# Two-layer encoder trunk on one core: the third weight sum of each Strassen block made by an adding DMA from GpSimd, one product moved, the engines' lists ordered anew

## The chip, the cores and the metric

The kernel runs on one core of a Trainium2 chip. The metric is the device time of one execution in microseconds. Engines: PE (TensorE), DVE (VectorE), ACT (ScalarE), POOL (GpSimd), and SP (SyncE), which issues nearly all DMAs. All weights are read from HBM in float32.

## The reference, cut to what matters

```python
def _swiglu(h, w_gate, w_up, w_down):
    return (jax.nn.silu(h @ w_gate) * (h @ w_up)) @ w_down

for l in range(DEPTH):                       # DEPTH = 2
    x = x + 0.5 * _swiglu(_rms_norm(x, ffn1_norm[l]), ffn1_w_gate[l], ffn1_w_up[l], ffn1_w_down[l])
    h = _rms_norm(x, mix_norm[l])
    ...                                      # convolution branch and attention branch, gated sum, w_out
    x = x + 0.5 * _swiglu(_rms_norm(x, ffn2_norm[l]), ffn2_w_gate[l], ffn2_w_up[l], ffn2_w_down[l])
return x
```

x is 256 x 1024; w_gate and w_up are 1024 x 2816, w_down is 2816 x 1024. There are four such feed-forward nets (FFNs), two in each layer, with the mixer between the two of a layer. The change touches the FFNs alone. The mixer matters here for one thing: attention needs the sine and cosine of positions times frequencies (the rotary key), and its RMS norm needs a root.

## The kernel before, in words

**Precision.** A product of float32 matrices is made of three passes on PE (`products`): the high part of the left with the high part of the right, high with low, low with high. So each weight unit (128 partitions x 2048 floats, 1 MB) is first split: ACT writes its rounded copy `whi` (`rounded`, line 1344), then DVE writes the remainder `wlo` = raw - `whi` (`remainder`, line 1854). A unit on PE is 24 matmuls of 512 columns for each 128 rows of x with gate/up weights, 12 + 12 with a down unit, 12 for a block product.

**Units and rings.** The units of a layer have one fixed order (`FFN_UNITS`, from `PRODUCTS`); `whi_ready`, `wlo_ready` and `unit_free` count them in this order. `whi` and `wlo` are rings of 6 units, `raw`, into which SP loads, is a ring of 3 (`place` waits until the unit three loads earlier is split, and `summed` for sums that still read it).

**An FFN** runs over 11 chunks of 256 hidden columns. A plain chunk c is `gate_up(c, 0)`, `gate_up(c, 1)` (two row tiles), and the down products of chunk c - 2. Chunks 4, 5 and chunks 7, 8 are done as one *block* each, in Strassen's way, with seven half-size products instead of eight: `strassen(4)` and `strassen(7)`. Its weights are quarters of w_gate and w_up: B11 (upper half of w_gate), an upper quarter of w_up, B22 (lower half of w_up), B21 (lower half of w_gate). DVE makes the sums T1 = B11 + upper w_up, T2 = T1 + B22, T3 = upper w_up + B22, T4 = T2 + B21 in place in two buffers, `chain[0]` (T1, T2, T4; it shares memory with `htok`) and `chain[1]` (T3; with `heads`), by `add` at line 2002. A sum is then split like any unit (`sum_of` on ACT, `of_chain` on DVE). The order of products on PE was B11, down of chunk c - 2, T1, T2, B22, B21, T3, T4, down of chunk c - 1.

**Order.** Each engine runs its list of steps in order; the lists of SP, ACT and DVE are written out by hand in each engine's `ffn` (SP from line 585, ACT from 1543, DVE from 2090), and every step waits on semaphores. `silu`, `mul`, `split_planes`, the transposing DMA `turn`, `join`, `round_joined` and `rest_joined` bring a chunk's hidden values from gate/up to the operand of its down product; `keep`, `up_first`, `gate_first` and their like gather a block's products.

**POOL** has in the FFNs only the roots of the norms (`root`, line 697, in `norm(l, n)`) and, in the first FFN of each layer, the range reduction for sine and cosine: 16 products (line 722) and 34 further steps, each followed by a small product (line 715) behind a wait. After these comes `norm(l, 1)`, the two roots of the mixer's norm. On DVE `norm_apply(l, 1, 0)` (line 1902) waits for the first of them, and behind it in DVE's list stands `mul(10, 1)` (line 1963), for which the last chunk's transposes on PE (`turn`, line 1028) wait.

Of the kernel before, what the change touches and what calls it, by code (L numbers as in the profile page):

```python
# [17 lines left out]
ALU = mybir.AluOpType  # L18
# [8 lines left out]
P = 128  # L27
# [6 lines left out]
FC = 256  # L34
# [25 lines left out]
PRODUCTS = ("B11", "D0", "T1", "T2", "B22", "B21", "T3", "T4", "D1")  # L60
# [32 lines left out]
SUM = {"T1": 1, "T2": 1, "T3": 1, "T4": 1}  # L93
# [77 lines left out]
def trunk(nc, a):  # L171
    with ExitStack() as ctx:
# [286 lines left out]

        block = ctx.enter_context(nc.Block())  # L460

        @block.sync
        def _(sp):
            def summed(l, u):
# [29 lines left out]

            def quarter_of(w, l, c, h):

                return w[l, 4 * h * P:4 * (h + 1) * P, c * FC:c * FC + CW].rearrange("(k p) n -> p k n", p=P)
# [68 lines left out]
            def ffn(l, f):  # L566
# [43 lines left out]
                lower_load(l, f, 4, "B22")  # L610
                turn(2)
                lower_load(l, f, 4, "B21")
# [11 lines left out]
                turn(5)  # L624
                turn(6)
                down(l, f, 6)
# [6 lines left out]
                down(l, f, 8)  # L633
                turn(8)
                down(l, f, 9)
                turn(9)
                down(l, f, 10)
# [50 lines left out]
        def _(pool):  # L688
# [14 lines left out]

            for l in range(DEPTH):
                norm(l, 0)

# [114 lines left out]
                norm(l, 2)  # L821


        @block.tensor
        def _(pe):
# [45 lines left out]
            def ffn(l, f):  # L871
# [45 lines left out]
                def strassen(c):  # L917
# [422 lines left out]
        def _(act):  # L1340
# [92 lines left out]
            def ffn(l, f):  # L1433
# [103 lines left out]
                silu(1, 0)  # L1537
                down_split(0)
                silu(1, 1)
# [6 lines left out]
                gate_split(3, 1)  # L1546
                down_split(1)
                round_joined(1)
                split_planes(2, 0)
                first_of(4, "B11")  # L1550
                silu(2, 1)
                split_planes(2, 1)
                down_split(2)
                sum_of(4, "T1")
                silu(3, 0)
                round_joined(2)
                silu(3, 1)
# [3 lines left out]
                split_planes(3, 0)  # L1561
                split_planes(3, 1)
                lower(4, "B21")
                sum_of(4, "T3")
                keep(4, 1, "T1")
                sum_of(4, "T4")
                keep(4, 2, "T2")
                down_split(3)
                gate_split(6, 0)
                round_joined(3)  # L1570
                keep(4, 3, "T3")
                block_silu(4, 0)
                gate_split(6, 1)
                split_planes(4, 0)
                block_silu(4, 1)
# [13 lines left out]
                sum_of(7, "T2")  # L1589
                keep(7, 0, "B11")  # L1590
                lower(7, "B22")
# [926 lines left out]
```

## Time and profile before

| | |
|---|---|
| median of 3 runs | 1025.89 us (1024.97, 1025.89, 1027.45) |
| profiled execution | 1025.66 us, span 1023.9 us |
| PE busy | 1018.2 us (99%), 4905 matmuls |
| DVE busy | 846.4 us (83%) |
| ACT busy | 660.8 us (65%) |
| POOL busy | 330.8 us (32%) |
| granted PE clock | 1.00 in every slice |
| HBM read | 192.9 MB, 189 GB/s over the span |

The profiled execution takes 1.8 us beside its span, and lies 0.2 us under the median. A matmul's start is recorded, its end is modelled, and each starts before the one ahead of it has ended; the distance between starts is what a matmul costs. "Idle before" is an engine's idle time ahead of a group with the releaser that ended it.

### The profile page before, as it was taken

To read this page: it belongs to the slowest core of one execution; us is meant where nothing else is said; L and a number is where in the kernel's file an instruction comes from. 1 tells how busy PE (TensorE), PEld (TensorE's weight loads), DVE (VectorE), ACT (ScalarE), POOL (GpSimd) and SP (SyncE) were. 2 spreads that over 40 slices of the span, in tenths; PEclk is the share of its full clock that TensorE was granted. 3 is DMA by queue.
4 is the path that set the end of the run, shared out by engine and by line. 5 is a ranking of instruction groups with operands and counts; after the bars stand their busy time and mean duration, and the time that the engine had idled before them with its cause. 6 is when DMAs were issued, how large, how long until landed. Compare 5 with 4: busy or idle time off the path is not lost.

```text
span 1023.9 us, 13331 instructions
## 1 busy us (share of the span) xinstructions
PE 1018.2 (99%) x4905; PEld 853.9 (83%) x4905; DVE 846.4 (83%) x1008; ACT 660.8 (65%) x836; POOL 330.8 (32%) x258
## 2 busy tenths in 40 slices
PE   9999999999999999999999999999999999999998
PEld 6888888998888888888888888889988888888887
DVE  6999977698976898888679889866999678988972
ACT  6767665576874575766557666647778556666761
POOL 2999400138850100000049990001589300000000
PEclk9999999999999999999999999999999999999999
DMA  8968578555544596748749574975366365947491
GB/s 278 309 191 277 162 209 274 160 185 176 207 161 128 182 328 183 244 140 234 228 154 339 166 226 135 274 248 174 127 214 226 123 173 185 331 140 233 158 240 42
DMA packets 175185, 208.99 MB, mean 204 GB/s; under 512 B 64112, under 2 KB 129936, under 8 KB 175120
## 3 DMA queue, kind: packets, MB, share of 16 engines
q1 hardware_dynamic: 173904, 206.03, 64.9%
q10 hardware_dynamic: 1216, 2.11, 0.7%
q8 instruction: 39, 0.64, 0.2%
q14 instruction: 26, 0.21, 0.1%
HBM read 192.90 MB, written 1.05 MB: 189 GB/s over the span
## 4 chain that ended last, share of the span: by engine, by line
PE 98%; ACT 1%; DVE 1%; DMA 0%; issue 0%; POOL 0%; ACTq 0%
PE bank L829 30%; PE bank L831 30%; PE bank L830 30%; PE bank L966 1%; PE bank L1128 1%; PE bank L1137 1%; PE bank L1158 1%; PE bank L868 0%; PE bank L1136 0%; PE bank L1160 0%; PE bank L836 0%; DMA cacc<-in_ffn_norm 0%; DVE htok L1902 0%; DVE x L1950 0%; ACT htok L1357 0%; PE bank L1146 0%
## 5 line engine op out<-in xcount | busy, mean ns | idle before, releaser
L1854 DVE TENSOR_TENSOR wlo<-raw,whi 128x2048 fp32r<-128x2048 f32 (+2 forms) x136 | 308.9, 2283 | 21.0 <-ACT whi L1344 21.0
L1344 ACT ACTIVATE whi<-raw 128x2048 fp32r<-128x2048 f32 (+2 forms) x160 | 302.9, 1910 | 25.3 <-DMA raw<-in_ffn_w_down 16.5
L829 PE MATMUL bank<-whi,hThi 128*128 128x512 f32 (+1 forms) x816 | 316.1, 387 | 0.0
L831 PE MATMUL bank<-whi,hTlo 128*128 128x512 f32 (+1 forms) x816 | 311.4, 382 | 0.0
L830 PE MATMUL bank<-wlo,hThi 128*128 128x512 f32 (+1 forms) x816 | 311.3, 381 | 0.0
L697 POOL TENSOR_TENSOR small<-small,expo 128x1 f32<-128x1 f32 (+3 forms) x20 | 30.0, 1505 | 470.5 <-DVE small L1895 432.9
L831 PEld LDWEIGHTS bank<-whi,hTlo 128*128 128x128 f32 x816 | 153.2, 188 | 29.6
L829 PEld LDWEIGHTS bank<-whi,hThi 128*128 128x128 f32 x816 | 153.3, 188 | 28.8
L830 PEld LDWEIGHTS bank<-wlo,hThi 128*128 128x128 f32 x816 | 153.4, 188 | 28.4
L829 PE MATMUL bank<-whi,gThi 128*128 128x512 f32 (+1 forms) x416 | 162.3, 390 | 0.0
L831 PE MATMUL bank<-whi,gTlo 128*128 128x512 f32 (+1 forms) x416 | 161.2, 388 | 0.0
L830 PE MATMUL bank<-wlo,gThi 128*128 128x512 f32 (+1 forms) x416 | 161.1, 387 | 0.0
L811 POOL TENSOR_TENSOR wlo<-raw,whi 128x2048 fp32r<-128x2048 f32 x24 | 110.1, 4608 | 21.1 <-ACT whi L1344 21.0
L2233 DVE SCALAR_TENSOR_TENSOR bank<-shared,vec,bank 128x256 f32<-128x256 f32 x240 | 98.1, 478 | 0.2
L831 PEld LDWEIGHTS bank<-whi,gTlo 128*128 128x128 f32 x416 | 78.1, 188 | 16.1
L829 PEld LDWEIGHTS bank<-whi,gThi 128*128 128x128 f32 x416 | 78.1, 188 | 15.8 <-issue 0.3
L830 PEld LDWEIGHTS bank<-wlo,gThi 128*128 128x128 f32 x416 | 78.2, 188 | 15.5
L1854 DVE TENSOR_TENSOR wlo<-htok,whi 128x2048 fp32r<-128x2048 f32 x32 | 73.2, 2287 | 10.7 <-ACT whi L1344 10.7
L715 POOL TENSOR_TENSOR small<-expo 128x1 f32<-128x1 f32 x72 | 75.0, 1041 | 5.9
L1344 ACT ACTIVATE whi<-htok 128x2048 fp32r<-128x2048 f32 x32 | 61.2, 1911 | 22.1 <-DVE htok L2002 17.4
L1497 ACT ACTIVATE qkT<-gates 128x512 uint16<-128x512 uint16 x80 | 48.5, 623 | 29.9 <-DVE gates L1963 14.8
L1458 ACT ACTIVATE gates<-bank 128x512 f32<-128x512 f32 x32 | 19.1, 596 | 61.6 <-PE bank L831 61.6
(201 smaller groups left out, 1359.0 us busy)
## 6 DMA issues: line engine op xcount, KB each, us to landing
raw<-in_ffn_w_down SPq DMA_DIRECT2D x88, 512.0 KB, 4.7
raw<-in_ffn_w_gate SPq DMA_DIRECT2D x68, 512.0 KB, 4.2
raw<-in_ffn_w_up SPq DMA_DIRECT2D x68, 512.0 KB, 5.2
raw<-in_w_in SPq DMA_DIRECT2D x48, 512.0 KB, 4.9
htok<-in_ffn_w_gate SPq DMA_DIRECT2D x16, 512.0 KB, 6.1
heads<-in_ffn_w_up SPq DMA_DIRECT2D x16, 512.0 KB, 6.8
raw<-in_w_out SPq DMA_DIRECT2D x16, 512.0 KB, 4.6
raw<-in_w_in SPq DMA_DIRECT2D x8, 544.0 KB, 5.2
```

The source lines that it names most:

```text
L697: return nc.gpsimd.tensor_tensor(out, in_, expo[:, :].to_broadcast([P, out.shape[-1]]), ALU.pow)
L715: nc.gpsimd.tensor_tensor(small[:, 95:96], expo[:, :], expo[:, :], ALU.mult)
L811: nc.gpsimd.tensor_tensor(wlo[:, slot(u, RING), 0:n], raw[:, raw_slot(l, u), 0:n], whi[:, slot(u, RING), 0:n].bitcast(F32), ALU.subtract). ...
L829: nc.tensor.matmul(out, lh, rh, start=start, stop=False, skip_group_check=skip)
L830: nc.tensor.matmul(out, lh, rl, start=False, stop=False, skip_group_check=skip)
L831: return nc.tensor.matmul(out, ll, rh, start=False, stop=stop, skip_group_check=skip)
L966: ins = nc.tensor.matmul(bank[:, 4 + t, :], left[:, 4 * h + k, t * P:(t + 1) * P], view(right, h, 2048, 4)[:, k, :], start=first and (h, k ...
L1344: nc.scalar.activation(whi[:, slot(u, RING), 0:USED[u]], src, ACT.Copy).then_inc(whi_ready, 1)
L1458: nc.scalar.activation(kept[(0, 2, 1, 3)[i]], bank[:, 5 if i == 1 else 4, :], ACT.Copy).then_inc(kept_ready, 1)
L1497: nc.scalar.activation(planes[:, :, :, t, :], words, ACT.Copy).then_inc(planes_ready, 1)
L1854: nc.vector.tensor_tensor(wlo[:, slot(u, RING), 0:n], src, whi[:, slot(u, RING), 0:n].bitcast(F32), ALU.subtract).then_inc(wlo_ready, 1)
L2233: ins = nc.vector.scalar_tensor_tensor(out=o, in0=i, scalar=w, in1=o, op0=ALU.mult, op1=ALU.add)
```

## The change

The sum T3 moves from DVE to a DMA that adds to its destination. POOL, once the upper quarter of w_up has landed in `chain[1]` and T1 (which reads it) is made, issues two DMAs of 512 KB, which read the lower half of w_up from HBM a second time and add it to `chain[1]`. `sum_ready["T3"]` then counts 32 for each block, and SP no longer waits for T3 before it reuses the place of B22. In POOL's list the waits and issues of both blocks stand directly behind the roots of the FFN's norm, and so ahead of the range reduction. On PE the T1 product goes ahead of the down product of chunk c - 2, and the two change places in the order of units. The lists of SP, ACT and DVE are in a new order. The diff, cut:

```diff
-PRODUCTS = ("B11", "D0", "T1", "T2", "B22", "B21", "T3", "T4", "D1")
+PRODUCTS = ("B11", "T1", "D0", "T2", "B22", "B21", "T3", "T4", "D1")
...
-SUM = {"T1": 1, "T2": 1, "T3": 1, "T4": 1}
+SUM = {"T1": 1, "T2": 1, "T3": 32, "T4": 1}
...
@@ SP, summed @@
                 if name == "B22":
                     sp.wait_ge(sum_ready["T2"], per_block(l, f, c))
-                    sp.wait_ge(sum_ready["T3"], per_block(l, f, c))
@@ SP, list of the FFN (chunks 2 to 4; the rest is reordered alike) @@
                 down(l, f, 0)
+                gate_up(l, f, 3, 0)
+                chain_load(l, f, 4, 0)
                 turn(0)
-                gate_up(l, f, 3, 0)
                 gate_up(l, f, 3, 1)
+                turn(1)
                 down(l, f, 1)
-                turn(1)
-                chain_load(l, f, 4, 0)
                 chain_load(l, f, 4, 1)
...
                 gate_up(l, f, 6, 1)
+                chain_load(l, f, 7, 0)
+                down(l, f, 4)
+                turn(4)
                 chain_load(l, f, 7, 1)
-                down(l, f, 4)
-                chain_load(l, f, 7, 0)
-                turn(4)
                 down(l, f, 5)
@@ POOL @@
+            def add_rows(l, f, c, name):
+
+                done = per_block(l, f, c)
+                if name == "T3":
+                    pool.wait_ge(chain_landed[1], done * 32)
+                    pool.wait_ge(sum_ready["T1"], done)
+                    dst, src = chain[1], quarter_of(wu[f], l, c, 1)
+                dst = dst.rearrange("p (k n) -> p k n", k=4)
+                for k in (0, 2):
+                    nc.gpsimd.dma_start(dst[:, k:k + 2, :], src[:, k:k + 2, :],
+                                        accum_op=ALU.add).then_inc(sum_ready[name], 16)
+
+            def sums(l, f):
+
+                add_rows(l, f, 4, "T3")
+                add_rows(l, f, 7, "T3")
+
             for l in range(DEPTH):
                 norm(l, 0)
+                sums(l, 0)
...
                 norm(l, 2)
+                sums(l, 1)
@@ PE, strassen @@
-                    down(c - 2, 0)
-                    down(c - 2, 1)
                     if c == BLK[0]:
                         pe.wait_ge(mixed_ready, l * 2 + f + 1)
                     block_product(c, "T1", 5, mixed_T(1, 1))
+                    down(c - 2, 0)
+                    down(c - 2, 1)
@@ ACT, list of the FFN @@
                 if (l, f) != (0, 0):
                     gate_split(1, 0)
+                    silu(0, 0)
                     gate_split(1, 1)
                     norm_squares(l, 2 * f, 1)
+                    silu(0, 1)
                     gate_split(2, 0)
-                    silu(0, 0)
-                    silu(0, 1)
                 split_planes(0, 0)
                 split_planes(0, 1)
                 gate_split(2, 1)
                 silu(1, 0)
+                silu(1, 1)
                 down_split(0)
-                silu(1, 1)
...
                 silu(6, 0)
-                down_split(5)
                 sum_of(7, "T1")
                 silu(6, 1)
+                round_joined(5)
+                down_split(5)
+                sum_of(7, "T2")
+                lower(7, "B22")
+                keep(7, 0, "B11")
                 split_planes(6, 0)
-                round_joined(5)
+                keep(7, 1, "T1")
+                lower(7, "B21")
                 split_planes(6, 1)
...
@@ DVE @@
-                def add_T3(c):
-                    dve.wait_ge(sum_ready["T1"], per_block(l, f, c) * SUM["T1"])
-                    add(c, "T3", lower_raw(c, "B22"))
...
                 mixed_rows()
+                mul(1, 0)
                 gate_split(2, 1)
                 join(0)
+                rest_joined(0)
+                mul(1, 1)
                 down_split(0)
-                mul(1, 0)
-                mul(1, 1)
-                rest_joined(0)
...
                 of_chain(7, "B11")
+                mul(6, 0)
                 add_T1(7)
                 rest_joined(4)
-                down_split(5)
-                mul(6, 0)
-                mul(6, 1)
                 join(5)
                 of_chain(7, "T1")
+                add_T2(7)
                 rest_joined(5)
-                add_T2(7)
-                add_T3(7)
+                mul(6, 1)
+                down_split(5)
                 of_chain(7, "T2")
                 lower(7, "B22")
+                lower(7, "B21")
                 add_T4(7)
-                lower(7, "B21")
                 of_chain(7, "T3")
```

## Rows read from the trace of the kernel before

**Rows 1.** page, parts 1 and 2: busy time and clock of the span

```profile
PE 1018.2 (99%) x4905; PEld 853.9 (83%) x4905; DVE 846.4 (83%) x1008; ACT 660.8 (65%) x836; POOL 330.8 (32%) x258
...
PEclk9999999999999999999999999999999999999999
```

**Rows 2.** who PE waited for: us in total, times, longest

```profile
PE bank L836 <- DVE zero L2432: 1.2, 1, 1.2
```

**Rows 3.** timeline of PE in block 7, first FFN: start us, us, line, operation

```profile
105.87 0.39 PE L829 MATMUL bank<-whi,gThi 128*128 128x512 f32 x1
...
114.03 0.39 PE L829 MATMUL bank<-whi,gThi 128*128 128x512 f32 x1
...
130.35 0.39 PE L829 MATMUL bank<-whi,sThi 128*128 128x512 f32 x1
```

**Rows 4.** groups of DVE by form: busy us, mean ns, idle before

```profile
L2002 DVE TENSOR_TENSOR heads<-heads,raw 128x2048 f32<-128x2048 f32 x8 | 18.3, 2281 | 0.0
```

**Rows 5.** timeline of DVE in the first FFN, around block 7

```profile
99.83 2.29 DVE L2002 TENSOR_TENSOR htok<-htok,heads 128x2048 f32<-128x2048 f32 x1
102.03 0.69 DVE L1861 TENSOR_TENSOR gTlo<-gates,gThi 128x512 fp32r<-128x512 f32 x1
```

**Rows 6.** timeline of ACT in the same stretch

```profile
100.63 0.47 ACT L1443 ACTIVATE gates<-bank,small 128x256 f32<-128x256 f32 x1 [1.83 <-PE bank L831]
101.00 1.91 ACT L1344 ACTIVATE whi<-raw 128x2048 fp32r<-128x2048 f32 x1
```

**Rows 7.** DMA issues: KB each, median us to landing

```profile
heads<-in_ffn_w_up SPq DMA_DIRECT2D x16, 512.0 KB, 6.8
```

**Rows 8.** timeline of POOL: the range reductions, and the roots behind them

```profile
22.25 0.19 POOL L720 CAST small<-posi 128x2 f32<-128x2 int32 x1
...
89.15 0.25 POOL L735 TENSOR_TENSOR ang<-ang 128x32 f32<-128x32 f32 x1
...
91.46 0.75 POOL L735 TENSOR_TENSOR ang<-ang 128x32 f32<-128x32 f32 x1
...
112.95 2.10 POOL L715 TENSOR_TENSOR small<-expo 128x1 f32<-128x1 f32 x1
174.28 0.57 POOL L697 TENSOR_TENSOR small<-small,expo 128x1 f32<-128x1 f32 x1 [59.23 <-DVE small L1895]
...
679.54 0.57 POOL L697 TENSOR_TENSOR small<-small,expo 128x1 f32<-128x1 f32 x1 [63.72 <-DVE small L1895]
```

**Rows 9.** windows: PE, PEld, DVE, ACT, POOL busy us (instructions), clock, DMA share, GB/s

```profile
22.00:44.00 22.00, 22.00 (x99) 18.21 (x98) 21.26 (x19) 17.43 (x19) 20.98 (x20) 1.00 0.96 280
44.00:115.00 71.00, 71.00 (x315) 58.80 (x314) 66.04 (x46) 45.14 (x44) 66.99 (x68) 1.00 0.74 239
106.00:140.00 34.00, 34.00 (x152) 28.15 (x151) 31.71 (x23) 21.82 (x21) 8.58 (x10) 1.00 0.47 146
140.00:174.30 34.30, 34.30 (x154) 28.37 (x153) 24.64 (x20) 19.93 (x21) 0.02 (x1) 1.00 0.97 289
...
611.00:646.00 35.00, 35.00 (x156) 29.00 (x155) 32.35 (x23) 22.56 (x22) 4.43 (x9) 1.00 0.49 151
646.00:679.50 33.50, 33.50 (x150) 27.69 (x150) 23.91 (x20) 19.19 (x20) 0.00 (x0) 1.00 0.93 289
```

**Rows 10.** timelines of DVE and PE at the end of the first FFN

```profile
177.75 0.48 DVE L1963 SCALAR_TENSOR_TENSOR gates<-bank,small,gates 128x256 f32<-128x256 f32 x1 [1.58 <-ACT gates L1443]
...
179.57 0.38 PE L1028 MATMUL bank<-ident,gates 128*128 128x128 f32 x2
```

**Rows 11.** timelines of ACT, DVE and PE, start of the second FFN

```profile
354.14 0.47 ACT L1443 ACTIVATE gates<-bank,small 128x256 f32<-128x256 f32 x1 [2.31 <-POOL small L697]
...
356.53 2.61 DVE L2034 TENSOR_TENSOR gates<-gates 128x512 f32<-128x512 f32 x4
359.12 2.29 DVE L1854 TENSOR_TENSOR wlo<-raw,whi 128x2048 fp32r<-128x2048 f32 x1
...
364.87 0.39 PE L829 MATMUL bank<-whi,hThi 128*128 128x512 f32 x1
```

More of the change, by code:

```diff
@@ L610, in ffn @@
                 lower_load(l, f, 4, "B22")
+                lower_load(l, f, 4, "B21")
                 turn(2)
-                lower_load(l, f, 4, "B21")
                 down(l, f, 3)
@@ L624, in ffn @@
                 turn(5)
+                down(l, f, 6)
                 turn(6)
-                down(l, f, 6)
                 gate_up(l, f, 9, 0)
@@ L633, in ffn @@
                 down(l, f, 8)
+                down(l, f, 9)
                 turn(8)
-                down(l, f, 9)
+                down(l, f, 10)
                 turn(9)
-                down(l, f, 10)
             def block_of(l, u, w, r0, k, c0, n):
@@ L1546, in ffn @@
                 gate_split(3, 1)
+                round_joined(1)
                 down_split(1)
-                round_joined(1)
+                silu(2, 1)
                 split_planes(2, 0)
                 first_of(4, "B11")
-                silu(2, 1)
                 split_planes(2, 1)
+                silu(3, 0)
+                sum_of(4, "T1")
+                split_planes(3, 0)
+                silu(3, 1)
+                round_joined(2)
                 down_split(2)
[L1554 to L1557, printed above, removed]
                 sum_of(4, "T2")
@@ L1582, in ffn @@
                 silu(6, 0)
[L1583 removed]
                 sum_of(7, "T1")
                 silu(6, 1)
+                round_joined(5)
[3 more added lines that the diff above has]
+                keep(7, 0, "B11")
                 split_planes(6, 0)
[L1587 removed]
+                keep(7, 1, "T1")
+                lower(7, "B21")
                 split_planes(6, 1)
[L1589 to L1592 removed]
                 sum_of(7, "T3")
[L1594 removed]
+                sum_of(7, "T4")
                 keep(7, 2, "T2")
[L1596 removed]
                 down_split(6)
+                round_joined(6)
                 gate_split(9, 0)
[L1599 removed]
+                gate_split(9, 1)
                 keep(7, 3, "T3")
                 block_silu(7, 0)
[L1602 removed]
                 block_silu(7, 1)
@@ L1606, in ffn @@
                 down_split(7)
+                gate_split(10, 0)
                 split_planes(8, 0)
+                silu(9, 0)
                 split_planes(8, 1)
                 round_joined(7)
-                gate_split(10, 0)
-                silu(9, 0)
                 gate_split(10, 1)
                 silu(9, 1)
+                down_split(8)
                 split_planes(9, 0)
                 split_planes(9, 1)
-                down_split(8)
+                down_split(9)
                 round_joined(8)
-                down_split(9)
                 c = NCH - 1
@@ L2135, in ffn @@
                 of_chain(4, "T3")
+                of_chain(4, "T4")
                 join(3)
-                of_chain(4, "T4")
-                up_first(4)
                 down_split(3)
                 rest_joined(3)
+                gate_split(6, 0)
+                up_first(4)
                 gate_first(4)
-                gate_split(6, 0)
+                block_mul(4, 0)
                 up_second(4)
-                block_mul(4, 0)
                 gate_second(4)
@@ L2167, in ffn @@
                 of_chain(7, "T4")
-                gate_first(7)
                 down_split(6)
                 rest_joined(6)
+                up_first(7)
+                gate_split(9, 0)
                 up_second(7)
-                gate_split(9, 0)
+                gate_first(7)
                 gate_second(7)
-                up_first(7)
                 block_mul(7, 0)
@@ L2178, in ffn @@
                 down_split(7)
+                gate_split(10, 0)
                 join(7)
+                mul(9, 0)
                 rest_joined(7)
-                gate_split(10, 0)
-                mul(9, 0)
+                gate_split(10, 1)
                 mul(9, 1)
                 join(8)
-                gate_split(10, 1)
-                rest_joined(8)
                 down_split(8)
                 down_split(9)
+                rest_joined(8)
                 c = NCH - 1
```

43 lines of the change are left out of this document (18 added, 25 removed).

## Prediction, made before the changed kernel was run

> **What bounds the kernel now.** I read the busy times first, then who PE waited for, then the distances between PE's starts, then the slack of each thing that PE consumes in the stretch that is changed.
>
> PE is busy 1018.2 of 1023.9 us at the full clock [rows 1]. PE's own list of waits has three entries, each a single wait in the first 15 us of the kernel; the longest is 1.2 us [rows 2]. So the question in each FFN is whether its matmuls start at their own pace or are stretched. In block 7 of the first FFN, PE starts the down products of chunk 4 at 105.87, the next product but one at 114.03, T3 at 130.35 [rows 3]. Between the first and the last lie 24 (down 4) + 12 (B11) + 24 (down 5) + 12 (T1) + 12 (T2) + 12 (B22) + 12 (B21) = 108 matmuls of 512 columns: (130.35 - 105.87) / 108 = 0.2267 us each. From 105.87 to 114.03 it is 8.16 / 36 = 0.2267 us: the same pace to the last digit. PE has no gap there, whatever DVE, ACT and the DMAs do. The windows of the first and third FFN say the same: 315 matmuls in 71.00 us, 152 in 34.00, 156 in 35.00 [rows 9] are 0.224 to 0.225 us each (one that crosses an edge counts in full); a stretch with a stall of 1 us would hold 4 fewer. The change takes no matmul away and adds none. What it can give back from the FFNs is nothing; all that it can do is to make something late that now is in time. That decides the sign, and the rest of this text asks for lateness.
>
> **The change part by part.**
>
> *Eight sums leave DVE.* They are 8 instructions of 2.281 us, 18.3 us in all [rows 4]. PE waited for none of them, so they are worth 0. They come back as time in which DVE waits for PE.
>
> *T3 by DMA, and when it has to be there.* Take block 7, the tighter one. DVE adds T1 from 99.83 on [rows 5], right behind the remainder of B11. In the new list `mul(6, 0)` stands ahead of it, and needs the `silu` that ACT makes at 100.63 for 0.47 us [rows 6], because PE has only then finished the products. So: silu done 101.1, mul (0.48, [rows 10]) 101.6, T1 (2.29) 103.9. `rest_joined(4)` behind it takes 0.69 [rows 5], to 104.6; PE wants it at 105.87 [rows 3]: 1.2 us to spare, no stall. The T3 product stays at 130.35, because T1 and the down product ahead of it only change places. Before it lie the remainder on DVE (2.28) and the rounding on ACT (1.91, [rows 6]): T3 must have landed by 130.35 - 2.28 - 1.91 - 0.1 = 126.1. Nothing at all moves if it has landed when ACT gets there; working ACT's and DVE's new lists forward with these durations gives 120. From T1 at 103.9 that is 16 us free of any effect and 22 us until PE waits. In block 4 the same working gives T1 at 54.5 and windows of 18 and 25 us.
>
> How long do the two adding DMAs take? No row shows one, nor any DMA from POOL. The nearest is the plain load of the same 512 KB into the same buffer: 6.8 us from issue to landing [rows 7], median of 16. Lower end: both overlap as the plain ones do, 7 to 8 us. Upper end: the destination is read as well as written, and the two run one after the other at double the time: 4 x 6.8 = 27 us, 5 us more than PE's limit in block 7 and 2 more in block 4. I take 8 to 14, nearer the plain load, since the 16 DMA engines are less than half busy there (share 0.47 from 106 to 140 us, [rows 9]). Cost 0; at the upper end 4 x (5 + 2) = 28 us.
>
> The Trainium skill ("DMA: Bandwidth & Descriptors", section "Anatomy of one DMA — SWDGE (gpsimd) path") gives 2.0 us + bytes / 436e3 for one DMA from GpSimd, an estimate of 3.2 us for 512 KB; it says nothing of an adding one. By it T3 would be in time as well.
>
> *POOL's list: what the new waits hold up.* This is the part with a price. The issues stand ahead of the range reduction, and the second pair waits for T1 of block 7. So in layer 1 the reduction no longer starts at 22.25 but at about 103.9 + 2 issues. A DMA issue on POOL is in no row: at least about 0, like POOL's short operations, at most the 6.8 us of a whole load [rows 7], if POOL were held until the data have landed. I take 1 us, nearer the short end, because an issue only describes the transfer. Start 106. The reduction took from 22.25 to 115.05, 92.8 us [rows 8]. Moved by its whole length it would end at 199, 25 us after the root that now starts at 174.28 [rows 8]. That would stall DVE at `norm_apply`, then `mul(10, 1)`, then PE.
>
> But its length isn't fixed. Its operations take 2.1 us beside a long DVE operation (112.95, as long as the 2.28 us that DVE holds) and 0.29 us when DVE is idle or reads PSUM: eight starts from 89.15 to 91.46 [rows 8]. Count by windows [rows 9]: from 22 to 115 POOL did 20 + 68 = 88 operations while DVE did 19 + 46 = 65 and was idle 0.74 + 4.96 = 5.70 us. 5.70 / 0.29 = 20 operations in idle time, the other 68 are 1.05 for each DVE operation. Now the new place, 106 to 174.3: DVE does 23 + 20 = 43 operations and is idle 2.29 + 9.66 = 11.95 us, giving 45 + 41 = 86 operations. T3's add, now gone from there, gives 2.28 / 0.29 - 1.05 = 7 more: 93, where 88 are needed. The reduction ends some 3 us before its root is due. In layer 2 everything comes 505.3 us later (root at 679.54 for 174.28, [rows 8]): start 611, DVE 43 operations and 2.65 + 9.59 = 12.24 us idle to 679.5 [rows 9], 45 + 42 + 7 = 94 for 89. So the cover holds, but it is thin: 5 operations. Behind it come 1.34 us of slack: `mul(10, 1)` ends at 178.23, PE wants it at 179.57 [rows 10]. Later than that each operation still missing costs 0.29 us, since DVE then stands still and no longer holds POOL up.
>
> The Trainium skill ("SBUF — State Buffer", section "Who interferes with whom") has the rule behind these rows: DVE and GpSimd share one port pair, held for a whole instruction, a DVE operation with two SBUF inputs shutting out a GpSimd operation that reads SBUF; the 2.1 us beside 0.29 us agree. The same page speaks against the change: GpSimd writes the descriptors of its DMAs itself, and is locked out while DVE runs in a two-port mode. If that held for each long operation, an issue would wait one of them out.
>
> *The orders.* T1 before down 5: T1 is wanted at 114.03 [rows 3]; forward from 103.9, ACT rounds it to 105.9 and DVE has the remainder at 108.1, 5.9 us early. The down product goes back by 2.72 us, so its unit and operand have more time. The tightest place that I find is the second half of chunk 2's weights in FFNs 2 to 4. Now: mixed rows to 359.1, remainder from 359.12 to 361.41, wanted by PE at 364.87 [rows 11]. New: silu to 354.61 (bound by POOL's root, [rows 11]), then `gate_split(2, 0)` on ACT to 356.5 and on DVE to 358.8, mul 359.2, mixed rows (2.61) 361.8, mul(1, 0) 362.5, remainder 364.8. It is ready 0.1 us before PE wants it. I charge 0.1 us for each of four FFNs, 0.4 in all; 0 to 2 is possible. SP's list: it loses one wait and no load of it moves by more than a few us; the last down unit is now asked for ahead of a transpose, which helps slightly and off the path.
>
> Sum: 0 (sums) + 0 (DMA) + 0 (POOL) + 0.4 (order) on the profiled 1025.66 us gives 1026.1; on the median, 0.2 us higher, 1026.3. I say 1026.2.
>
> **The rivals.**
>
> *POOL is late (slower).* The point from which it decides: 5 operations of surplus and 1.34 / 0.29 = 4.6 of slack, at 0.94 operations per us in the stretch from 106 to 140 (32 in 34 us), is 10 us. If the two issues of block 7 hold POOL for more than about 12 us, near the upper end of 2 x 6.8, PE stalls at the end of the first FFN of each layer. For 20 us: (18 x 0.94 - 9.6) x 0.29 = 2.1 us a layer, 4 in all: 1030. If each issue had to wait out one long DVE operation (2.28 us), the pair would take 6.6 us and stay under the point. Chance 0.09.
>
> *T3 lands late (slower).* From 22 us after T1 on. At the upper end, +28 us: 1054; a few us beyond the limit in block 7 alone, +4 to +12: 1034. Against it: a share of the DMA engines of 0.47. Chance 0.07.
>
> *The new lists starve PE somewhere (slower).* 0.1 us of spare at chunk 2, 1.2 us at `rest_joined(4)`. Half a microsecond short in each FFN at two places gives 4 us: 1030. Chance 0.07.
>
> *DVE was the bound after all (faster).* Then 18 us come back: 1008. Against it speaks the even 0.2267 us. Chance 0.02; another 0.01 for less than that.
>
> **How the numbers follow.** A measurement of this kernel can tell about 0.2% (2 us) from no change. Forecast case 0.74, 1025 to 1028, which is within 0.2% of 1025.89. The three slower rivals have 0.23. Faster by over 0.2%: 0.03; within: 0.74; slower: 0.23. The range reaches from 1024.8 (the lowest run of before less a little) up to 1030.5, which takes in the late POOL and short stalls and leaves out the late T3.
>
> **What would show each step.** The remaining DVE additions are 24 instead of 32, and DVE's busy time falls by 18 us with the end unmoved. PE's starts stay at 0.2267 us through both blocks. ACT's wait for T3 is short or absent; the POOL operations run from about 106 to about 172 us, more of them at 0.2 to 0.3 us, and the root behind them starts at 174.3. If instead `norm_apply` (line 1902) waits longer for POOL in the list of waits than now, POOL is late; if line 1344 waits for a DMA ahead of T3, the sum is late; if PE shows waits for `wlo` at chunk 2, it is the lists. A PE pace other than 0.2267 us in the FFNs would overturn the whole argument.

## The result, and the profile after

The changed kernel takes 1052.37 us (median of 4 runs, 1049.15 to 1055.2) beside 1025.43 us for the kernel before on the same chip: a ratio of 1.0259, 95% interval 1.0241 to 1.0276. It is 26.9 us slower, where 1026.2 and no change that can be measured was forecast, and it lies far outside the range. Its profiled run took 1051.78 us, of which the span is 1050.0, 26.1 us more than before; this span is taken apart below. In the comparisons that follow, one execution of e4 (2082 us) and one of the kernel before (1128 us) fell in a slow state, and the ratios are made without them. The page of the profiled run, to be held against [rows 1]:

```profile
span 1050.0 us, 13343 instructions
PE 1028.5 (98%) x4905; PEld 856.9 (82%) x4905; DVE 829.6 (79%) x1000; ACT 660.5 (63%) x836; POOL 300.7 (29%) x274
PEclk9999999999999999989999999999999999999999
PE 50%; POOL 13%; DVE 13%; DMA 10%; issue 7%; ACT 5%; SPq 2%; ACTq 0%; DVEq 0%; POOLq 0%
```

DVE lost 17 us of work, as the change meant, and the end came 26 us later. The chain of work that ended last (the last line) is only half PE now, with DMA, DVE and POOL in it. PE is still "98% busy", since its idle time rose only from 5.7 to 21.5 us; its busy time rose too, by 10.3 us, of which half is a slower pace (below). The list of waits says more. For PE, where [rows 2] had nothing beyond the start:

```profile
PE bank L847 <- DVE gTlo L1879: 8.7, 4, 2.5
PE bank L847 <- DVE wlo L1872: 5.2, 4, 3.1
PE bank L886 <- DVE htok L1920: 1.9, 2, 1.2
```

And for those PE waits for (us in total, times, longest):

```profile
DVE gates L1996 <- DMA qkT<-qkT: 52.8, 16, 9.8
ACT gThi L1523 <- DVE gates L1996: 51.6, 18, 8.6
POOL heads L712 <- issue: 49.4, 8, 10.5
```

The first of these stood at 3.6 us in 4 times, 1.3 at the longest, in the kernel before (its line was 1978 there). `join` (line 1996) waits for the transposing DMA `turn`, then ACT waits for `join`, then PE for DVE's remainder.

**Where the 26.1 us of span lie.** I summed what PE's starts lie further apart than 0.2267 us, over all matmuls of 512 columns. Eleven starts (one is that of a transpose on PE between two of them) came over 0.3 us late, 16.4 us together (none before). Behind the first 8 us, 46 starts stand 0.35 to 0.5 us apart, where the kernel before has 16: 5.9 us more. The two waits at the mixer's norm are 1.9 us. That makes 24.2 of 26.1 us; the rest is spread thin. The loss comes FFN by FFN: 6.7, 8.3, 6.6 and 4.6 us.

The first chunk shows how it starts. SP's list in the first FFN, the kernel before and then the changed one:

```profile
26.63 1.34 SPq L537 DMA_TRANSPOSE qkT<-qkT  x1
29.99 0.39 SPq L484 DMA_DIRECT2D raw<-in_ffn_w_gate  x1
```

```profile
30.29 0.38 SPq L487 DMA_DIRECT2D raw<-in_ffn_w_gate  x1
30.71 0.51 SPq L487 DMA_DIRECT2D raw<-in_ffn_w_up  x1
31.27 1.02 SPq L512 DMA_DIRECT2D htok<-in_ffn_w_gate  x2
32.40 1.67 SPq L536 DMA_TRANSPOSE qkT<-qkT  x1
```

The load `gate_up(3, 0)` can't go before 30 us in either kernel, because its place of `raw` isn't free. The transpose now stands behind it, and goes at 32.40 rather than 26.63. It also lands behind 2 MB of loads just issued: 7.3 us after its issue rather than 4.9. In the kernel before it landed at 31.54 and `join(0)` was made at 34.62, without a wait. DVE, in order:

```profile
39.72 0.76 DVE L1996 COPY gates<-qkT 128x1024 uint16<-128x1024 uint16 x1 [4.33 <-DMA qkT<-qkT]
...
63.76 0.76 DVE L1996 COPY gates<-qkT 128x1024 uint16<-128x1024 uint16 x1 [2.72 <-DMA qkT<-qkT]
...
73.60 0.68 DVE L1879 TENSOR_TENSOR gTlo<-gates,gThi 128x512 fp32r<-128x512 f32 x1
```

Chunks 0 and 2 are joined late. From 63.76 on DVE works without a gap, and the remainder of chunk 2 (`rest_joined`, 73.60), with five steps of its list between it and the join, comes when PE has run dry:

```profile
71.80 0.39 PE L849 MATMUL bank<-whi,sTlo 128*128 128x512 f32 x1
74.34 0.50 PE L847 MATMUL bank<-whi,gThi 128*128 128x512 f32 x1 [2.15 <-DVE gTlo L1879]
...
75.85 0.63 PE L847 MATMUL bank<-whi,gThi 128*128 128x512 f32 x1
76.27 0.63 PE L848 MATMUL bank<-wlo,gThi 128*128 128x512 f32 x1
```

After the stall the starts go on at about 0.23 us apart for 1.5 us, and then stand 0.427 us apart for eight matmuls. From 75.8 to 80 us the granted clock was 0.59; the eight are at the lower of PE's two clock levels, 1.2 GHz. The worst place is block 7 of the second FFN, where `join(5)` waits longest and PE then runs at half clock (windows: PE busy and count, clock, DMA share, GB/s):

```profile
452.72 0.74 DVE L1996 COPY gates<-qkT 128x1024 uint16<-128x1024 uint16 x1 [9.80 <-DMA qkT<-qkT]
```

```profile
456.00:462.00 6.00, 5.94 (x15) 0.54 0.54 87
462.00:480.00 18.00, 18.00 (x81) 1.00 0.71 217
```

The clock costs 26 such matmuls x 0.2 = 5.2 us of the 26.1; they are most of the 5.9 us above.

**POOL.** Its two pairs of adding DMAs in the first FFN, the start of the reduction, and the root behind it:

```profile
60.70 1.35 POOL L712 DMA_DIRECT2D heads<-in_ffn_w_up  x1 [38.13 <-DVE htok L2020]
67.01 1.23 POOL L712 DMA_DIRECT2D heads<-in_ffn_w_up  x1 [4.96 <-issue]
110.04 1.22 POOL L712 DMA_DIRECT2D heads<-in_ffn_w_up  x1 [41.80 <-DVE htok L2020]
117.72 1.23 POOL L712 DMA_DIRECT2D heads<-in_ffn_w_up  x1 [6.46 <-issue]
118.47 0.82 POOL L737 CAST small<-posi 128x2 f32<-128x2 int32 x1
...
181.62 0.57 POOL L696 TENSOR_TENSOR small<-small,expo 128x1 f32<-128x1 f32 x1
```

An issue costs 1.2 us, but the second stands still until the first has landed (110.04 + 7.3 = 117.3, then 117.72; at 443.00 in the second FFN the first took 11.4 us, and the second went at 454.72). The reduction took 63 us from 118.5 to 181.6, in place of the 92.8 us of [rows 8].

### The profile page after: what moved, and what is told of

Read it like the earlier page. It is cut to its first block, busy times and chain, and to the rows that moved or that the text cites. A ratio compares the mean times of both kernels' runs of the same rounds, so it can differ in the third digit from the quotient of the medians.

```text
span 1050.0 us, 13343 instructions
## 1 busy us (share of the span) xinstructions
PE 1028.5 (98%) x4905; PEld 856.9 (82%) x4905; DVE 829.6 (79%) x1000; ACT 660.5 (63%) x836; POOL 300.7 (29%) x274
## 4 chain that ended last, share of the span: by engine, by line
PE 50%; POOL 13%; DVE 13%; DMA 10%; issue 7%; ACT 5%; SPq 2%; ACTq 0%; DVEq 0%; POOLq 0%
PE bank L847 15%; PE bank L848 15%; PE bank L849 15%; DMA qkT<-qkT 8%; DVE wlo L1872 7%; POOL ang L739 4%; POOL small L732 4%; ACT whi L1362 2%; DMA raw<-in_ffn_w_down 2%; DVE htok L2020 2%; POOL ang L751 2%; POOL small L696 1%; SPq L487 1%; POOL ang L752 1%; ACT qkT L1515 1%
## 5 line engine op out<-in xcount | busy, mean ns | idle before, releaser
L847 PE MATMUL bank<-whi,gThi 128*128 128x512 f32 (+1 forms) x416 | 165.0, 397 | 10.9 <-DVE gTlo L1879 8.7
L712 POOL DMA_DIRECT2D heads<-in_ffn_w_up x16 | 19.8, 1239 | 356.7 <-DVE htok L2020 307.3
L849 PEld LDWEIGHTS bank<-whi,gTlo 128*128 128x128 f32 x416 | 79.0, 190 | 16.8
L1996 DVE COPY gates<-qkT 128x1024 uint16<-128x1024 uint16 x40 | 30.2, 754 | 53.2 <-DMA qkT<-qkT 52.8
L1461 ACT ACTIVATE gates<-bank,small 128x256 f32<-128x256 f32 x56 | 26.3, 470 | 58.5 <-PE bank L849 45.5
```

Of the source, the lines that this page charges most:

```text
L847: nc.tensor.matmul(out, lh, rh, start=start, stop=False, skip_group_check=skip)
L849: return nc.tensor.matmul(out, ll, rh, start=False, stop=stop, skip_group_check=skip)
L1461: nc.scalar.activation(sgate[:, t, :], gu_bank(c, t)[:, 0:FC], ACT.Silu, scale=rs[:, t:t + 1]).then_inc(silu_ready, 1)
L1996: nc.vector.tensor_copy(g_turned.bitcast(U16).rearrange("p (n b) -> p b n", b=2), turned.rearrange("p (b j) r -> p b (j r)", b=2)).then_in ...
```

## The experiments

All times are medians. The kernel before measured 1025.3 to 1025.9 us in these comparisons.

**Which part costs.** Theory S: transposes behind loads in SP's list. Theory D: the adding DMA. Theory P: the new place of T1 with the new lists of ACT and DVE. Four kernels, the first being the changed kernel with SP's old list:

```diff
 # SP's list, after -> e1 (all its lines as before), for instance
-                gate_up(l, f, 3, 0)
-                chain_load(l, f, 4, 0)
                 turn(0)
+                gate_up(l, f, 3, 0)
```

> The changed kernel with SP's list of the kernel before: each transposing DMA is issued again ahead of the loads that the change put in front of it; all else as changed. Theory S (the transposes land late because SP issues them behind 1 to 3 MB of loads, DVE's join waits for them, and its lists pass the lateness on to PE): DVE's wait for the transposes falls from 52.8 us to under 15, PE's waits from about 16 us to under 4, time 1026 to 1032 us. Theory D (the adding DMA takes the DMA engines from the transposes): still 1045 to 1055. Theory P (T1 ahead of the down product, or the new lists of ACT and DVE, are too tight by themselves): 1040 or more.

Measured: 1028.19 us, ratio 1.0020 (1.0010 to 1.0029). DVE's wait for the transposes fell from 52.8 to 19.3 us (under 15 was expected), and PE waits only in the start. The execution whose trace is kept took 1026.30 us, the shortest of ten, so it doesn't show where the 2.5 us of the median lie.

The second is the reverse, the kernel before with the changed list of SP and nothing else:

> The kernel before with nothing changed but SP's list, taken from the changed kernel. Theory S: join waits for the transposes as in the changed kernel (tens of us in sum), PE starves in block 4 and 7, time 1038 to 1055 us. Theories D and P: no adding DMA and no moved product here, so 1025 to 1028.

Measured: 1048.52 us, 1.0217 (1.0193 to 1.0241). So the list alone, without an adding DMA and with every product in its old place, costs 22.9 us. But these are not the changed kernel's stalls. Added over the four FFNs, PE's starts fall behind those of the kernel before by 2.9 us up to the end of block 7 (24.0 in the changed kernel) and by 16.9 us from there to the FFN's end (2.4 in the changed kernel). What PE waits for most is `mul(10, 1)`, ahead of the last chunk's transposes on PE:

```profile
PE bank L1028 <- DVE gates L1963: 9.2, 4, 2.5
```

Ahead of it DVE stood 4.6 us in the first FFN for the transposing DMA of chunk 8, which the new list also puts behind a load. So e2 shows that SP's list alone makes transposes late and costs time; that it costs nearly the same time is luck. The third is the DMA alone:

```diff
 # before -> e3: add_rows and sums on POOL as in the change, and on DVE
-                add_T3(4)
-                add_T3(7)
```

> The kernel before with T3 made by POOL's two adding DMAs, the waits and issues ahead of the range reduction as in the change; T3's add is gone from DVE; all lists otherwise and PE's order as before. Theory S: nothing is late, 1025 to 1028 us, the first root of the mixer's norm late by 0 to 3 us at most. Theory D: the transposes are late here too, 1038 to 1052.

Measured: 1025.72 us, 0.9999 (0.9989 to 1.0009). Theory D falls, and 18 us less work on DVE bring nothing, as PE was dense. ACT waited twice for the adding DMA ahead of T3, 0.6 and 0.8 us, without any effect on PE. Its POOL:

```profile
103.02 1.22 POOL L712 DMA_DIRECT2D heads<-in_ffn_w_up  x1 [37.48 <-DVE htok L2020]
110.05 1.23 POOL L712 DMA_DIRECT2D heads<-in_ffn_w_up  x1 [5.82 <-issue]
...
172.69 0.19 POOL L732 TENSOR_TENSOR small<-expo 128x1 f32<-128x1 f32 x1
174.60 0.57 POOL L696 TENSOR_TENSOR small<-small,expo 128x1 f32<-128x1 f32 x1 [1.72 <-DVE small L1913]
```

The reduction ends 1.7 us before its root. The fourth is the changed kernel with T3 back on DVE:

```diff
 # after -> e4
-                sums(l, 0)
-                sums(l, 1)
+                add_T3(4)      # DVE, behind down_split(2), ahead of rest_joined(2)
+                add_T3(7)      # DVE, behind down_split(5)
```

> The changed kernel with T3 added by DVE again (ahead of the remainder of T2), no DMA from POOL; SP's list and all else as changed. Theory S: still 1045 to 1060 us. Theory D: 1026 to 1032.

Measured: 1060.93 us, 1.0333 (1.0316 to 1.0350), 8.6 us above the changed kernel and just above what either theory had. Once the transposes are late, taking the sum off DVE is worth 8.6 us; the same is worth nothing in e3. Most of it can be read at one place: the add of 2.28 us stands here ahead of `rest_joined(2)`, which in the kernel before was ahead of it, and PE's waits for that remainder grow from 8.7 us (2.5 at the longest) to 16.5 (4.3). No run has the add behind it, so what the DMA is worth with the better order stays open.

The other half of theory P, T1 ahead of the down product in the kernel before:

> Edit: the kernel before, with the T1 product ahead of the down product of chunk c - 2 on PE and in the order of units, and only those steps of ACT's and DVE's lists exchanged that this order asks for; SP's list of the FFN as before, T3 on DVE. Theory S (only the transposes' place in SP's list costs): T1 is wanted 24 matmuls (5.4 us) earlier and the spare shrinks from there, PE keeps 0.2267 us: 1025 to 1027. Rival P (T1 is too early for the old list of DVE, where its sum stands behind other steps): a stall of 0.5 to 2 us in each of 8 blocks, 1029 to 1040, seen as a wait of PE for wlo ahead of the product with gThi of mixed rows.

Measured: 1025.48 us, 0.9998 (0.9989 to 1.0007): no cost that can be measured.

**Which transposes.** In the changed list those of chunks 0 and 2 stand behind loads that they were ahead of. That of chunk 5 has the same loads ahead of it as before, but `chain_load(7, 1)` has moved from ahead of `turn(4)` to behind it, so that 4 MB rather than 3 MB are issued between the two transposes. Each was put back alone, then all three:

```diff
 # after -> f1                          # after -> f2
+                turn(0)                -                lower_load(l, f, 4, "B21")
                 gate_up(l, f, 3, 0)                     turn(2)
                 chain_load(l, f, 4, 0) +                lower_load(l, f, 4, "B21")
-                turn(0)
 # after -> f3: chain_load(l, f, 7, 1) to ahead of down(4), chain_load(l, f, 7, 0) to behind it;
 # turn(4) and turn(5) then stand behind the same loads as before
 # f4: f1, f2 and f3 together
```

> Edit: the changed kernel, but in SP's list the transposing DMA of chunk 0 goes ahead of the two loads behind which it now waits. Everything else, the later transposes among it, stays as changed. Theory S (each transpose issued behind loads brings its own lateness): the transpose is issued near 26.6 us again instead of 32.4 and lands in about 5 us, join(0) no longer waits, and the stall of 1.0 us near 43.5 us goes together with its slow matmuls: 3 to 8 us of the 26 come back, 1044 to 1049. Theory L (lateness is inherited: what is late at chunk 0 makes chunks 2 and 5 late): nearly all comes back, 1027 to 1034. Theory O (chunk 0 is harmless, 2 and 5 carry it): 1050 to 1053.

> Edit: the changed kernel, but the transposing DMA of chunk 2 goes ahead of the load of B21 of block 4 again, behind B22's alone. Theory S: its landing falls from 7.6 to about 4.6 us, the stall of 2.3 us near 71.8 us in the first FFN (and the like in the other three) goes or shrinks to below 1 us: 6 to 12 us come back, 1040 to 1046. Theory L: next to nothing comes back, since the lateness starts at chunk 0: 1048 to 1053.

> Edit: the changed kernel, but the two chain loads of block 7 have their old places and order in SP's list (1 ahead of down(4), 0 behind it), so that the transposes of chunks 4 and 5 are not behind the second of them. Theory S: chunk 5's transpose lands in 7 to 9 us rather than 9.5 to 14, and the stall of 3.3 us near 452 us shrinks: 4 to 12 us come back, 1040 to 1048. Theory L: 1048 to 1053. A rival in this place alone: the landing of chunk 5's transpose is set by the two down units and by POOL's adding DMA, not by the chain load; then under 3 us come back.

> Edit: the three edits on SP's list together; all other places of the changed list (turn(1) ahead of down(1), turn(6) behind down(6), turn(8), turn(9), turn(7)) stay as changed. Theory S: these three transposes carry the loss: 1027 to 1032. If it comes out above 1036, other places of SP's list count as well, and which is to be read from the transposes' landings. If the sum of what the three give back one by one is well below what they give together, a stall stays as long as any one of them is late (the lists pass it on); if it is above, they overlap.

Measured: f1 1037.69 (1.0111, 1.0095 to 1.0127), f2 1043.87 (1.0179, 1.0162 to 1.0195), f3 1039.38 (1.0127, 1.0099 to 1.0156), f4 1026.11 (1.0007, 0.9998 to 1.0017). The three carry all of the changed kernel's loss: with them back, and the adding DMA, the early T1, the new lists of ACT and DVE and the rest of SP's new list kept, the time is that of the kernel before. PE's waits in f4 are those of the start, and DVE's for transposes are short:

```profile
PE bank L854 <- DVE zero L2444: 1.2, 1, 1.2
```

```profile
DVE gates L1996 <- DMA qkT<-qkT: 12.0, 9, 2.7
```

f3 moves loads and not a transpose, so it could also have helped by bringing block 7's input earlier. Against that speaks the changed kernel's trace: every wait of DVE for a DMA that is longer than 0.5 us is for a transpose.

But f1 and f3 gave back more (14.7 and 13.0 us) than the 3 to 8 and 4 to 12 that theory S had for them, and the three one by one give 36 where there are 26. So prices of single transposes don't add up. Three more runs put one late at a time, on f4:

> Edit: the changed kernel with the transposes of chunks 2 and 5 back and chunk 0's alone behind its two loads. Measured: (0, 2, 5 late) 1052.4; (2, 5) 1037.7; (0, 5) 1043.9; (0, 2) 1039.4; none 1026.1. If each late one had a price of its own, the three pairs give 9.7 for chunk 0, 3.5 for chunk 2 and 8.1 for chunk 5 (sum 21.3, not 26.3): 1035 to 1037 here. If one alone is taken up by slack, as in the kernel before (1026.4), 1026 to 1029, and what costs is two late within one FFN.

> Edit: the same with chunk 2's transpose alone behind the load of B21. Price of its own: 1029 to 1031. Taken up by slack: 1025.5 to 1027.5. In the run with (2, 5) late the stalls of PE are all at block 7 (from 445 us on) and none at block 4, where chunk 2's lateness would show; that speaks for slack.

> Edit: the same with the chain loads of block 7 as changed, so that chunk 5's transpose alone is behind both. Price of its own: 1033 to 1036, with the stalls at block 7 of the second FFN (2.3 and 2.5 us near 450 us) as in the run with (2, 5) late. Taken up by slack: 1026 to 1029.

Measured: chunk 0 alone 1028.79 (1.0030, 1.0018 to 1.0042), chunk 2 alone 1026.30 (1.0007, 0.9998 to 1.0016), chunk 5 alone 1033.72 (1.0091, 1.0066 to 1.0115; its runs scatter from 1030.3 to 1037.2, and the kept trace is that of the shortest). With these all eight combinations are there, in us over f4 by the medians (they come from several comparisons, whose kernel before differed by up to 0.6 us):

| late | none | 2 | 0 | 5 | 2, 5 | 0, 2 | 0, 5 | all |
|---|---|---|---|---|---|---|---|---|
| | 0 | 0.2 | 2.7 | 7.6 | 11.6 | 13.3 | 17.8 | 26.3 |

Chunks 0 and 2 cost 2.9 us singly and 13.3 together. The reason can be read from when chunk 2's transpose lands in the first FFN (issue plus landing) and PE's wait ahead of its down product:

| late | issued | landed | PE waits near 73 us |
|---|---|---|---|
| none | 52.00 | 56.6 | none |
| 2 | 51.46 | 58.9 | none |
| 0 | 55.93 | 60.6 | none |
| 0, 2 | 55.66 | 62.7 | 1.70 |
| all | 56.12 | 63.7 | 2.15 |

A late chunk 0 makes chunk 2 be issued 4 us later, since ACT and DVE run their lists in order; standing behind a load adds 2 to 3 us. Either fits into the slack, which ends between 60.6 and 62.7; both don't. The PE wait with 0 and 2 late (f3), one such in each FFN:

```profile
71.25 0.39 PE L849 MATMUL bank<-whi,sTlo 128*128 128x512 f32 x1
73.33 0.50 PE L847 MATMUL bank<-whi,gThi 128*128 128x512 f32 x1 [1.70 <-DVE gTlo L1879]
```

**Under the lists of before, and by which way a transpose is late.** One late transpose in the kernel before, and the changed kernel with one of the two loads ahead of it taken away:

```diff
 # before -> g1                          # after -> g2
-                turn(0)                                  gate_up(l, f, 3, 0)
                 gate_up(l, f, 3, 0)      -                chain_load(l, f, 4, 0)
+                chain_load(l, f, 4, 0)                    turn(0)
+                turn(0)                  +                chain_load(l, f, 4, 0)
# g1: the chain load comes from behind turn(1)
```

> Edit: the kernel before, with one thing taken from the change: in SP's list the transposing DMA of chunk 0 stands behind gate_up(3, 0) and behind the chain load of block 4 (which is asked for earlier by that). T3 stays on DVE, product order and ACT's and DVE's lists stay as before. Expected in any case: it is issued near 32 us rather than 26.6 and lands in 7 us or more rather than 4.9, and join(0) waits 3 to 5 us for it. Theory S1 (one late transpose is enough to stall PE, whatever the lists of ACT and DVE): 1029 to 1036. Theory S2 (one is taken up by the slack of the lists before, it takes several, or the new lists, to reach PE): 1025 to 1027.5, as the three late ones of the changed kernel, put right one by one, gave back 14.7, 8.5 and 13.0 us, 36 in all, where putting right all three gave 26.3.

> Edit: the changed kernel, with the chain load of block 4 moved from ahead of to behind the transposing DMA of chunk 0, so that only gate_up(3, 0) stands ahead of it. It parts two ways in which the transpose is late: its issue waits in SP's list until the load ahead of it may go (the place of raw is freed), and once issued its landing waits behind the load's bytes. If the wait in the list is the larger part, it is still issued near 31 us (31.3 less 1.0 for the two issues of the chain load) and most of the loss stays: 1045 to 1052. If the bytes are, it lands in 4 to 5 us rather than 7.3, is there 3 us earlier, and a good part of the 14.7 us that moving it back gave comes: 1040 to 1045.

Measured: g1 1026.38 (1.0006, 0.9997 to 1.0016). DVE's wait for transposes rose from 3.6 to 21.2 us, the longest to 5.8, and PE has one wait of 0.5 us from it. The old lists of ACT and DVE swallow what costs 2.7 us in the new. e2 says the same of all three late ones: 2.9 us up to the end of block 7, where the changed kernel loses 24.0. So most of the loss needs two things together: SP's new order, and the new lists of ACT and DVE with the early T1 (no run parts these two; the adding DMA isn't needed for it, as e4 loses more without it). g2 measured 1038.05 (1.0121, 1.0104 to 1.0138), as good as f1, and below the lower of my two expectations. In the first FFN its transpose is issued at 31.09, 1.3 us earlier than in the changed kernel, and lands in 6.1 us rather than 7.3, so it is there 2.5 us earlier. The landing of chunk 0's transpose in the second FFN, f4, g2 and the changed kernel, with no load, 1 MB and 2 MB issued right ahead of it:

```profile
DMA to landing us min/median/max: 3.1/3.1/3.1
```

```profile
DMA to landing us min/median/max: 5.1/5.1/5.1
```

```profile
DMA to landing us min/median/max: 7.0/7.0/7.0
```

So the landing takes 2 us more for each MB there. These 2 us and a little of the issue, at chunk 0 alone, give back 14.3 us of the loss.

**POOL's second issue.** f4 with T3 in quarters (`SUM["T3"]` is then 64):

```diff
-                for k in (0, 2):
-                    nc.gpsimd.dma_start(dst[:, k:k + 2, :], src[:, k:k + 2, :],
+                for k in range(4):
+                    nc.gpsimd.dma_start(dst[:, k:k + 1, :], src[:, k:k + 1, :],
```

> Edit: the changed kernel with the three transposes back (as in the run with all three, 1026.1), and T3's sum in four adding DMAs of 256 KB instead of two of 512 KB. Measured so far: with two, the second is issued 0.3 us after the first has landed (issue at 56.58, landing after 6.0, next issue at 62.85), so POOL stands still for 5 to 10 us. Rival W (an adding DMA waits until the one before it has landed, whatever its size): four issues with three such waits of some 3 to 5 us each, the four over in 12 to 20 us. Rival F (POOL may have a fixed amount in flight, which two halves exceed and three quarters don't): the first three issues follow each other at about 1 us, and only the fourth waits, until the first has landed; the four are over in 8 to 12 us. The time stays at 1025.5 to 1028 in either case, as T3 has some 16 us.

Measured: 1025.96 us, 1.0003 (0.9994 to 1.0013). Its POOL in the two blocks of the first FFN:

```profile
55.92 3.07 POOL L712 DMA_DIRECT2D heads<-in_ffn_w_up  x3 [33.52 <-DVE htok L2020]
64.46 0.89 POOL L712 DMA_DIRECT2D heads<-in_ffn_w_up  x1 [5.47 <-issue]
104.65 2.37 POOL L712 DMA_DIRECT2D heads<-in_ffn_w_up  x2 [39.30 <-DVE htok L2020]
111.29 0.86 POOL L712 DMA_DIRECT2D heads<-in_ffn_w_up  x1 [4.27 <-issue]
115.84 0.88 POOL L712 DMA_DIRECT2D heads<-in_ffn_w_up  x1 [3.69 <-issue]
```

Three of 256 KB went at once in block 4, two in block 7, and at 610.20 in the third FFN only one. Neither rival holds: W is wrong, since two or three can overlap, and F has no fixed number. What all cases share is that a held issue goes 0.2 to 0.4 us after the one just ahead has landed (104.65 and its follower landed by 111.0, the next went at 111.29). What decides whether an issue is held stays open. Quarters occupy POOL for 12.1 us in block 7, halves for 7.7 in f4: splitting finer holds POOL longer. ACT waited for quarters four times ahead of T3, 2.5 us at the longest, and PE did not.

## Why the prediction was wrong, point by point

**PE is dense, so the change can only make things late: right.** e3 took the 18 us of sums off DVE and measured 0.9999. The question that the text set itself, what gets late, was the right one.

**T3 by DMA in time: right.** The adding DMAs of the changed kernel land 5.9 us after issue (median of 16), and ACT never waited for them there or in f4. In f4 the second pair's data are there at 117.3 and ACT takes them at 120.19, 2.9 us later. The 8 to 14 us for a pair came out as 11.9 to 17.6 us in the changed kernel and 13.6 to 16.8 in e3. There the 16 us that the text gave T3 "free of any effect" were used up, as ACT's two waits show; the way to PE's limit was long enough. The Trainium skill ("DMA: Bandwidth & Descriptors", section "Anatomy of one DMA — SWDGE (gpsimd) path") would have it at 3.2 us, an estimate from its formula; the adding ones here are nearly twice as slow, and the measurement decides.

**POOL's list: the mechanism right, one term mis-sized.** "2 issues" at 1 us each was the term. An issue is 1.2 us, but a pair takes 7.7 us in f4 and up to 13 in the changed kernel, because the second is held. Whether DVE's long operations would hold an issue up was left open in the text, with a rule of the Trainium skill ("SBUF — State Buffer", section "Who interferes with whom") against the change. All 16 issues of the changed kernel take 1.21 to 1.35 us, eight of them beside a DVE operation of 2.28 us, so no run here shows such a lock-out. The other half, how the reduction's length follows DVE's idle time, held: in e3 it ended 1.7 us before its root where about 3 were forecast. In f4 the root starts at 174.95 right behind the reduction, with no slack left and no stall. In the changed kernel the root at 181.62 comes 1.5 us after what it waits for, that of layer 2 comes 1.9 us late, and PE's two waits at the mixer's norm (1.9 us) are behind them. The pair is longer than in f4 in layer 1 alone (8.9 us against 7.7; 7.9 in both in layer 2). In the stretch of the reduction DVE is idle for 9.5 us in each layer, against 11.4 and 10.3 us in f4, and POOL does 82 and 80 operations where f4 does 86 and 87. That fits the text's account of the reduction; no run parts it from the pair's length.

**The orders of products, ACT and DVE: right, as far as their inputs are in time.** e5 is at 0.9998, and f4, which has all of them, at 1026.11 where 1026.2 was forecast for the whole change. The remainder at chunk 2, forecast with 0.1 us to spare, was made without a wait of PE. What the forecast missed is that these lists have less slack for a late input: one late transpose costs 0.6 us under the old lists (g1, not to be told from nothing) and 2.7 under the new (i0), and all three 2.9 us up to the end of block 7 (e2) and 24.0.

**SP's list: the step that failed.** The text says that "no load of it moves by more than a few us" and that a down unit ahead of a transpose "helps slightly and off the path". It looked at the loads, and not at what the loads are put in front of. Of each reordering it should have asked when every transpose can be issued and when it lands. Both were to be had from the trace of before: `gate_up(3, 0)` went at 29.99, so a transpose behind it and the chain load can't go before 29.99 + 0.9 + 1.0 = 31.9 (it went at 32.40), and it shares the DMA engines with 2 MB issued just ahead, which in that trace take 4.2 to 6.8 us to land (medians of the loads from gate and up weights). So the transpose of chunk 0 is there at 36 to 39 rather than 31.5, and `join(0)`, made at 34.62 in the kernel before, is 1.5 to 4 us late; it came at 39.72, 5.1 late. DVE's and ACT's lists stand still behind it, and the same again at chunks 2 and 5. No rival named this mechanism. "The new lists starve PE" came nearest, but it was priced with the durations on ACT and DVE alone, at 4 us.

The Trainium skill has the rule ("DMA: Bandwidth & Descriptors", section "Queues, rings and completion order"): SP has one ring on each DMA engine, whose descriptors are taken up in ring order. So what SP issues later starts behind what it issued before, on each engine that both use. The three landings above, 3.1, 5.1 and 7.0 us, agree. It spoke against the change, and the text didn't weigh it.

**Size.** Even with the mechanism seen, adding prices up would have failed: single late transposes cost 10.5 us together and all three 26.3. The stalls of PE themselves also brought 5.2 us of half clock.

## What to carry to other kernels

In a queue that issues both bulk loads and small transfers on which a compute step waits, moving a load ahead of a small one delays it twice: by the load's own wait for a buffer, and by its bytes. Work out issue and landing for each small transfer before judging the order, and keep the small one ahead. Slack that takes up one late input doesn't take up two in a row in engines that run in list order, so neither a single-edit test nor a sum of single prices tells what a reordered list costs. Nor does the time of a list tried under the old lists of the other engines (e2) say where it will stall under the new ones. And work taken off an engine which PE never waits for is worth nothing until something else makes that engine late.

## What was not expected of the hardware

- The transposing DMA of chunk 0 in the second FFN lands in 3.1 us with no load issued right ahead, 5.1 behind 1 MB and 7.0 behind 2 MB. The longest landing of one was 14.0 us, in the second FFN, behind 4 MB of loads issued within 5 us and with an adding DMA from 443.00 on beside it (11.2 at that place in e4, which has no adding DMA). There SP's own issue took 5.29 us rather than 1.24.
- An adding DMA of 512 KB takes 1.2 us to issue on POOL and 5.9 to land (median in the changed kernel; 7.2 in e3), and the next one from POOL is held until it has: 5.7 us at the longest in f4 and 10.5 in the changed kernel.
- PE's granted clock fell to 0.54 in the stretch behind a 3.1 us stall. Behind the stall of 2.15 us the matmuls at half clock began only 1.5 us after PE had gone on; behind the stall of 3.1 us they began with the second matmul.
